# Rows of x2 for experts 2 to 31: fetched by indirect DMA from DRAM in place of selection on TensorE

## What is computed

```python
hn = rms_norm(x2, g)
g_prob = softmax(hn @ w_route_group + b_route_group); g_w, g_idx = top_k(g_prob, 1)
e_logits = (hn @ w_route_expert + b_route_expert).reshape(N, 4, 8)[arange(N), g_idx[:, 0]]
top_l, top_i = top_k(e_logits, 2)
comb = g_w * softmax(top_l)              # weights of the two experts of a row
eid = g_idx * 8 + top_i
# for each expert e and the rows xb that chose it:
y = (silu(xb @ w_gate[e]) * (xb @ w_up[e])) @ w_down[e]
out = x2 + sum over the two experts of y * comb
```

## Time and profile before

| | us |
|---|---|
| median of 3 runs | 989.34 (986.97 to 989.44) |
| profiled execution | 990.02 |
| its span | 987.9 |
| TensorE busy | 957.2 (97%) |
| VectorE busy | 405.5 (41%) |
| ScalarE busy | 245.5 (25%) |
| GpSimd busy | 58.5 (6%) |
| moved by DMA | 251.94 MB, mean 255 GB/s |

### The profile page before, as it was taken

The page is one execution under the profiler, slowest core; times in us unless marked ns, Lnnn a source line. Parts: engine busy times, 40 slices in busy tenths (PEclk is TensorE's granted clock), DMA queues, the critical chain, the costliest instruction groups (busy, mean ns, idle before and its releaser), DMA issues.

```text
span 987.9 us, 12620 instructions
## 1 busy us (share of the span) xinstructions
PE 957.2 (97%) x4944; PEld 520.3 (53%) x4944; DVE 405.5 (41%) x930; ACT 245.5 (25%) x607; POOL 58.5 (6%) x63
## 2 busy tenths in 40 slices
PE   5999999999999999999989999999999999999996
PEld 4554777777678888855453333333333333333332
DVE  4689688686543444562751241211211211111110
ACT  3432555355433100032212111111111111111110
POOL 0100000000000000001000101011101101101101
PEclk9999999999999999999999999999999999999998
DMA  9620412112112227288079999999999999999981
GB/s 327 212 86 20 151 63 74 44 49 81 43 43 86 85 86 275 88 334 342 33 268 370 417 418 406 417 417 421 421 416 419 424 415 418 422 419 417 426 329 17
DMA packets 32537, 251.94 MB, mean 255 GB/s; under 512 B 7784, under 2 KB 11112, under 8 KB 17480
## 3 DMA queue, kind: packets, MB, share of 16 engines
q1 hardware_dynamic: 28768, 242.19, 60.4%
q0 software_dynamic: 3712, 8.96, 3.6%
HBM read 244.08 MB, written 12.35 MB: 260 GB/s over the span
## 4 chain that ended last, share of the span: by engine, by line
PE 89%; DVE 6%; DMA 2%; ACT 1%; issue 1%; SPq 1%; POOL 0%; POOLq 0%; DVEq 0%; ACTq 0%
PE ps L1954 24%; PE ps L2258 21%; PE ps L2285 12%; PE ps L2198 10%; PE ps L1892 6%; PE ps L2113 4%; DMA arena<-in_x 2%; PE ps L2243 2%; PE ps L2268 1%; PE ps L2039 1%; PE ps L2013 1%; PE ps L1970 1%; PE ps L1996 1%; PE ps L2259 1%; PE ps L2147 1%
## 5 line engine op out<-in xcount | busy, mean ns | idle before, releaser
L1954 PE MATMUL ps<-arena 128*128 128x272 f32 x1120 | 266.7, 394 | 2.6 <-DVE arena L1368 1.0
L1954 PEld LDWEIGHTS ps<-arena 128*128 128x128 f32 x1120 | 209.0, 190 | 52.2 <-issue 7.0
L2259 PE MATMUL ps<-arena 128*64 128x512 f32 x512 | 226.5, 595 | 0.0
L2258 PE MATMUL ps<-arena 128*64 128x512 f32 x512 | 226.5, 595 | 0.0
L808 ACT ACTIVATE arena<-ps 128x272 f32<-128x272 f32 (+5 forms) x188 | 90.4, 487 | 387.6 <-PE ps L1954 168.4
L2258 PEld LDWEIGHTS ps<-arena 128*64 128x64 f32 x512 | 67.6, 137 | 126.5 <-issue 124.5
L2198 PE MATMUL ps<-arena 128*64 128x512 bf16 (+2 forms) x768 | 105.6, 424 | 2.9 <-DVE arena L1614 2.0
L1694 DVE SCALAR_TENSOR_TENSOR arena<-arena,list_w,ps 64x512 f32<-64x512 f32 x32 | 24.0, 749 | 201.5 <-ACT arena L1079 201.5
L1892 PE MATMUL ps<-arena 128*128 128x512 f32 (+1 forms) x192 | 74.9, 549 | 6.4 <-DVE arena L1160 6.4
L2198 PEld LDWEIGHTS ps<-arena 128*64 128x64 bf16 (+2 forms) x768 | 49.0, 117 | 52.3 <-issue 19.4
L1690 DVE TENSOR_TENSOR arena<-ps,g_ffn 128x512 f32<-128x512 f32 x32 | 22.1, 692 | 122.0 <-PE ps L2243 122.0
(11 more groups left out here) (258 smaller groups left out, 761.4 us busy)
## 6 DMA issues: line engine op xcount, KB each, us to landing
arena<-in_w_gu SPq DMA_DIRECT2D x62, 2048.0 KB, 16.7
arena<-in_w_ed SPq DMA_DIRECT2D x30, 2048.0 KB, 19.6
arena<-in_w_pair SPq DMA_DIRECT2D x20, 1024.0 KB, 4.9
arena<-in_w_q SPq DMA_DIRECT2D x2, 2048.0 KB, 15.5
arena<-in_w_out SPq DMA_DIRECT2D x2, 2048.0 KB, 12.3
arena<-in_w_ed SPq DMA_DIRECT2D x8, 512.0 KB, 14.1
arena<-in_w_gu SPq DMA_DIRECT2D x8, 512.0 KB, 17.3
arena<-in_x SPq DMA_DIRECT2D x4, 512.0 KB, 11.2
```

The source lines that it names most:

```text
L1954: ins = mm(out, w[:, k, :], tokens[:, k, :], start=k == 0 and q in "127", stop=k == 3, skip_group_check=q not in "127")
L2258: mm(ps[0:C, 2 + s, :], xT[s][:, j, :], w[:, jj, 1, :], start=j == 0, stop=j == JX - 1)
L2259: ins = mm(ps[64:64 + C, 2 + s, :], xT[s][:, j, :], w[:, jj, 0, :], start=j == 0, stop=j == JX - 1)
```

## The change

x2 is written a second time, to a DRAM tensor x2_rows, next to each store to y and by the same engine. For experts 2 to 31 the rows are fetched from it by an indirect DMA of GpSimd (gather_x) with the same list as the later add: 64 list entries, one row of 1024 values to one partition, entries beyond the list skipped. The two buffers x_rows lie on partitions 0 to 63 and 64 to 127 and are zeroed once. gather_x(2) and gather_x(3) are issued once all copies of x2 and the lists are there, gather_x(e + 4) in turn e of GpSimd's loop, once the rows of expert e + 2 have been transposed, before add_y(e). select_rows, hot_places and stage_x remain for experts 0 and 1 alone. turn_gathered transposes the 64 rows in eight steps of 128 columns in the place of turn_x's four. Semaphore counts follow; three semaphores are merged into zeros_set. The item loop still selects.

```diff
@@ -49,6 +49,7 @@
 NOBODY = 1024
 N_CHUNK = 10
 BIAS = 4096
+GATHERED = tuple(range(2, NE))
 UNROLL = 10
 MASKED = -1.0e30
 NEVER = -3.0e38
...
@@ -234,6 +235,7 @@
         hot = split(area(52608, 2 * (NT - 1) * C // 2).bitcast(BF16), (2, NT - 1, C))
         hot_last = area(52864, 2, C)
         mark_tmp = area(52992, NT, NE)
+        x_rows = [area(52992, D)[64 * s:64 * s + C, :] for s in range(2)]
 
 
         CHUNK_AT = [8192] + [19584 + 4096 * c for c in range(6)] + [0, 4096, 15488]
...
@@ -271,6 +273,8 @@
             at, n = CONST[name]
             return split(const[:, at:at + n], shape or (n,))
 
+        x2_rows = nc.dram_tensor("x2_rows", (T, D), F32, kind="Internal").ap()
+
         ident = cc("ident")
         before_bf, ones_bf = (cbf[:, n * P:(n + 1) * P] for n in range(2))
 
...
@@ -545,6 +548,10 @@
             upper, middle, lower = (split_rows[:, ORDER[j], n, c * 512:(c + 1) * 512] for n in range(3))
             return [(x_half(h), rest, upper, middle, lower)]
 
+        SELECTED = [e for e in range(NE) if e not in GATHERED]
+        N_SELECTED = len(SELECTED)
+        PER_ROUND = sum(UNROLL < e - 1 <= 2 * UNROLL for e in SELECTED)
+
         SELECT = [[(0, 0)]] + [[(j, n) for n in range(3)] for j in range(1, NT - 1)] + [[(NT - 1, 0)]]
 
         def x_bank(s):
...
@@ -588,9 +595,9 @@
         def base_written(eng):
 
             for b in range(4):
-                eng.wait_ge(half_moved[b], 48 if b < 3 else 16)
-            eng.wait_ge(last_written, 16)
-            eng.wait_ge(dec_written, 16)
+                eng.wait_ge(half_moved[b], 80 if b < 3 else 32)
+            eng.wait_ge(last_written, 32)
+            eng.wait_ge(dec_written, 32)
 
         block = ctx.enter_context(nc.Block())
 
...
@@ -682,6 +689,7 @@
             sp.wait_ge(out_ready, LAST + 1)
             load_chunk(EARLY + 1)
             sp.wait_ge(x2_ready, LAST + 1)
+            sp.dma_start(half_cols(x2_rows, LAST), x_half(LAST)).then_inc(last_written, 16)
             sp.dma_start(half_cols(o["y"], LAST), x_half(LAST)).then_inc(last_written, 16)
             load_chunk(N_CHUNK - 1)
 
...
@@ -755,17 +762,20 @@
             pool.wait_ge(c21_taken, 4)
             pool.dma_start(o["up_T"], uT[:, :, UP + SEQ - UP:UP + SEQ]).then_inc(nu_out, 16)
             pool.tensor_copy(split(u_decT.rearrange("p k n -> p (k n)"), (KD, DEC_B, DEC_S)),
-                             uT[:, :, UP + SEQ:].rearrange("p k (b u) -> p k b u", b=DEC_B)[:, :, :, UP:]).then_inc(u_dec_copied, 1)
-            pool.wait_ge(u_dec_copied, 1)
+                             uT[:, :, UP + SEQ:].rearrange("p k (b u) -> p k b u", b=DEC_B)[:, :, :, UP:]).then_inc(zeros_set, 1)
+            pool.wait_ge(zeros_set, 7)
             pool.dma_start(o["us_T"], u_decT).then_inc(nu_out, 16)
 
+            pool.memset(area(52992, D), 0.0).then_inc(zeros_set, 1)
             pool.wait_ge(x2_ready, 1)
+            pool.dma_start(x2_rows[SEQ:, :], x_dec[0:DEC, :]).then_inc(dec_written, 16)
             pool.dma_start(o["y"][SEQ:, :], x_dec[0:DEC, :]).then_inc(dec_written, 16)
             for h in range(1, LAST):
                 pool.wait_ge(x2_ready, h + 1)
+                pool.dma_start(half_cols(x2_rows, h), x_half(h)).then_inc(half_moved[(h - 1) % 4], 16)
                 pool.dma_start(half_cols(o["y"], h), x_half(h)).then_inc(half_moved[(h - 1) % 4], 16)
                 if 1 < h < 5:
-                    pool.wait_ge(half_moved[h - 2], 16)
+                    pool.wait_ge(half_moved[h - 2], 32)
                     pool.wait_ge(turned, h)
                     pool.wait_ge(ssq2_ready, h)
                     pool.wait_ge(parts_taken, h)
...
@@ -778,12 +788,22 @@
                     in_=y_rows[s][0:C, :], in_offset=None, compute_op=ALU.add,
                     bounds_check=T - 1, oob_is_err=False).then_inc(y_out[s], 16)
 
-            pool.wait_ge(dec_written, 16)
-            for bb in range(4):
-                pool.wait_ge(half_moved[bb], 48 if bb < 3 else 16)
-            pool.wait_ge(last_written, 16)
+            def gather_x(e):
+
+                pool.indirect_dma_start(
+                    out=x_rows[e % 2][0:C, :], out_offset=None, in_=x2_rows,
+                    in_offset=bass.IndirectOffsetOnAxis(ap=list_i[:, e:e + 1], axis=0),
+                    bounds_check=T - 1, oob_is_err=False).then_inc(x_full[e % 2], 16)
+
+            base_written(pool)
             pool.wait_ge(rows_listed, 1)
-            for e in range(NE):
+            pool.wait_ge(zeros_set, 8)
+            for e in range(-2, NE):
+                if e + 4 in GATHERED:
+                    above(pool, xe_ready, max([g + 1 for g in GATHERED if g < e + 4 and g % 2 == e % 2], default=0))
+                    gather_x(e + 4)
+                if e < 0:
+                    continue
                 for q in range(2):
                     pool.wait_ge(y_taken[q], e + 1)
                 above(pool, y_out[(e + 1) % 2], 16 * ((e + 1) // 2))
...
@@ -1088,18 +1108,24 @@
                 act.sem_inc(passed, 1)
                 copy(y_rows[s][0:C, 512:1024], ps[64:64 + C, 6 + s, :]).then_inc(y_taken[1], 1)
 
-            def stage_x(e, s, bank=0):
-
-                act.wait_ge(picked, e + 1)
-                above(act, xe_ready, e - 1)
-                copy(x_picked[s], ps[:, bank, :]).then_inc(x_staged, 1)
+            def stage_x(turn, free, bank=0, s=None):
+
+                act.wait_ge(picked, turn + 1)
+                above(act, xe_ready, free)
+                copy(x_picked[turn % 2 if s is None else s], ps[:, bank, :]).then_inc(x_staged, 1)
+
+            def stage(e):
+
+                turn = SELECTED.index(e)
+                stage_x(turn, SELECTED[turn - 2] + 1)
 
             stage_x(0, 0)
-            stage_x(1, 1, 3)
+            stage_x(1, 0, 3)
             do_silu(0, 0, root_of(0))
             take_hidT(0, 0)
             do_silu(1, 1, root_of(1))
-            stage_x(2, 0)
+            if 2 in SELECTED:
+                stage(2)
             base_written(act)
             take_y(0, 0, 0)
             for e in range(2, NE):
...
@@ -1703,11 +1730,12 @@
             def column(table, e):
                 return table[0:C, 0, e:e + 1] if isinstance(e, int) else table[0:C, 0, bass.ds(e, 1)]
 
-            def step(e, k, half, last=False):
+            def step(e, k, half, first=0, more=0, last=False):
 
                 s = k % 2
-                if not last and (not isinstance(e, int) or e > 1):
-                    hot_places(e + 1, 1 - s)
+                if not last and k + 1 + first in SELECTED:
+                    turn = SELECTED.index(k + 1 + first)
+                    hot_places(e + 1, turn + more, turn % 2)
                 if last:
                     take_y(e - 1, 1 - s, half - (1 - s))
                 hidden(e, s, column(list_w, e))
...
@@ -2234,14 +2263,28 @@
                 pe.wait_ge(sem, value)
                 pe.sem_inc(passed, 1)
 
-            def turn_x(e, s):
-
-
-                before_transposing(x_staged, e + 1)
-                rows = x_picked[s]
+            def turn_x(s, turn, part):
+
+
+                before_transposing(x_staged, turn + 1)
                 for j in range(JX // 2):
-                    ins = transpose(split(ps[:, x_bank(s), :], (2, JX // 2, C))[:, :, j, :], rows[:, j * P:(j + 1) * P], ident)
+                    ins = transpose(split(ps[:, x_bank(s), :], (2, JX // 2, C))[:, :, j, :], x_picked[part][:, j * P:(j + 1) * P], ident)
                 ins.then_inc(xe_ready, 1)
+
+            def turn_gathered(e, s):
+
+                pe.wait_ge(x_full[s], 16 * len([g for g in GATHERED if g <= e and g % 2 == s]))
+                rows, own = split(x_rows[s], (JX, P)), slice(64 * s, 64 * s + C)
+                for j in range(JX):
+                    ins = transpose(ps[:, x_bank(s), j * C:(j + 1) * C], rows[:, j, :], ident[own, own])
+                ins.then_inc(xe_ready, 1)
+
+            def turn_rows(e):
+
+                if e in GATHERED:
+                    turn_gathered(e, e % 2)
+                else:
+                    turn_x(e % 2, SELECTED.index(e), SELECTED.index(e) % 2)
 
             def gate_up(e, s, n, more):
 
...
@@ -2286,17 +2329,18 @@
                                  start=j == 0, stop=j == JH - 1)
                 ins.then_inc(dn_ready, 1)
 
-            turn_x(0, 0)
+            turn_rows(0)
             select(1, (NT - 1,), 3).then_inc(picked, 1)
             tile_list(NT - 1)
             gate_up(0, 0, up_no(0, 0), (0, 0))
             pe.wait_ge(rows_listed, 1)
-            turn_x(1, 1)
+            turn_rows(1)
             pe.wait_ge(hit_ready, NT + 1)
             list_rows(ps[0:C, 4, 0:2 * NE], 1, 2)
             gate_up(1, 1, up_no(1, 0), (0, 0))
             turn_hid(0, 0)
-            select_rows(2, 0)
+            if 2 in SELECTED:
+                select_rows(2, 0)
             for t in range(NT):
                 r = ROWS[t]
```

(50 more changed lines are left out.)

3 lines of the change are left out of this document (1 added, 2 removed).

## The result

The changed kernel takes 996.59 us (median of 4 runs, 995.62 to 997.55), the kernel before 988.89 us (4 runs, 986.97 to 989.44): a ratio of 1.0081, with the 95% interval 1.0062 to 1.0100. It is nearly 8 us slower. The forecast was 982.1 us, 7 us faster; the time lies outside the range of 978.5 to 991. The profiled execution took 995.84 us with a span of 994.0 us.

The account below looks back on a forecast made before the run. The weight stream was taken as the bound: its end, 961 - 1.0 (hole) + 9.6 (gathers) + 0.7 (add_y) = 970.3 us, plus the tail gave a span of 980.7 and a forecast of 982.1 us, range 978.5 to 991.

Parts of the forecast that it names:

- the lag: At the kernel's end: 20 us from the stream's last data to TensorE's last matmul, all a faster TensorE can win.
- TensorE's side: Expert loop: selection matmuls go, eight transposes take 0.78 us; an expert falls from 14.60 to 11.8 us.
- The gathers: Weight stream in the expert loop: 28 paid gathers at 0.34 us each move its end by 9.6 us.
- the bound above: Price of a gather in the expert loop: at most an indirect add's 0.73 us, 20.4 us for 28.
- Rival A: Expert loop: gathers dearer than their bytes, through uneven engine load or an add's cost; 992.9 us at the add's price; chance 0.25.
- Rival E: Expert loop: a gather is late or the additional queue traffic disturbs the weights; above 993 us; chance 0.05.
- The rule on accumulating transfers: Gather price: an accumulating transfer is half as fast as a copy, so a gather costs half an add, 0.36 us.
- The copies, the holes, the added waits: Before and early in the expert loop: copies cost 0, a closing hole gains 1.0 us, added waits cost nothing.
- The tail: After the last weight piece at 970.3 us: last matmuls end at 974.1 us, 6.65 us more to the span's end.
- Rival B: TensorE's clock falls while it waits for weights; a lag at the end of up to 4 us, 986 us; chance 0.12.
- C: Whole expert loop: the stream isn't the bound and TensorE's 84 us count in full, 905 us; chance 0.01.
- D: Kernel's end and expert loop: the tail runs at full clock and gathers sit more in gaps, 979 us; chance 0.05.

Follow-up runs that it names:

- e1_none: The changed kernel without the gathers for experts 4 to 31 (output not the layer's): 971.17 us, ratio 0.981 to the kernel before.
- e2_copies: The kernel before with only the second copy of x2 to DRAM added, nothing read from it: 988.59 us, ratio 0.9998.
- e6_spread: The changed kernel with each gather replaced by a plain load of 32 neighbouring rows, 1 KB to each of 128 partitions (wrong output): 979.2 us.
- e9_halves: The changed kernel with each gathered row sent as two half rows to partitions p and 64 + p, right output: 982.42 us, ratio 0.9931.

## Why the prediction was wrong

**What bounds the kernel.** Right. The weight stream was the slower resource, TensorE waits for it from about 620 us on (forecast 650; with the true 16.26 us per expert, 5.4 us a piece, the same working gives n = 32 and 637 us), and of 84 us taken from TensorE nothing was left beyond the lag.

**TensorE's side.** Right. Eight transposes take 0.64 us (forecast 0.78), an expert 11.7 us.

**The gathers: the term that failed.** "28 x 0.34 = 9.6 us". A gather cost not 0.34 us but 0.81 to 0.83 us, some 23 us in all, over the bound above of 20.4 us as well. The stream's end was forecast at 970.3 us and came at 984. Of the 13.7 us between, the gather's own engine time is a small part: 7.1% of 350 us less 22 adds at 0.73 us leaves 8.8 us for 22 gathers, 0.40 us each, if an add still takes what it took before; 28 x 0.06 = 1.7 us. The large part is what no term stood for, the weight packets beside it: (2.413 - 2.348) us per MB x 6.29 MB = 0.41 us per expert, 28 x 0.41 = 11.5 us. The sum so mended is 983.5 us. Per gather that is 0.81 us, and the ends say the same: 0.83 us from 984 - 961 + 1.0 - 0.7 over 28, 0.81 us from the last packets of the changed kernel and of e1_none, 984.6 - 962.0 over 28. The reasoning "less than its bytes it can't cost" was sound as a bound below. The bound above was not one: I took the price of an add as the worst, but an add writes to DRAM and takes its rows out of SBUF, and so could say nothing of writes into SBUF.

The Trainium skill ("SBUF — State Buffer", section "Door 1: The DMA port swizzle (why `[64,N]` ≈ `[32,N]`)") says that DMA bandwidth depends on how many of 16 ports the partitions reach, and that partitions 0 to 63 reach eight of them. The page says this of a transfer's own bandwidth. The runs fit it and go further, to the packets of the other queue: 633 ns beside loads to 32 partitions and 614 ns beside loads to 128. They show that the choice of partitions decides; that the two streams meet at the ports is an inference that no run here shows. Nor do they tell the number of partitions from the half in which they lie, since no load went to 32 partitions taken from both halves, or to all 64 of one; and the packet records don't name the DMA engine, so whether the slowed packets are those of some engines alone stays open.

**Rival A** had the right direction, place and turning point, and a chance of 0.25. It said that a gather over 0.60 us takes the gain away and over 0.70 us makes the kernel slower by more than 0.3%; it was 0.81 to 0.83 us, and 996.6 us came of it. Its mechanism was not this one. I looked for uneven load or a dear gather in q0's own time, and answered it with "the adds have the same shape and leave the total share at 1.01". The share is 1.01 after the change too, at 407 GB/s in the place of 418: here time in which packets are held up counts as busy, so the share can't show it. MB per share can. Of the signs of being wrong, this rival's came true (last data after 977 us, a period above 16 us).

**Rival E** named what happened, in one clause: "the additional queue traffic disturbs the weights: above 993 us". It had a chance of 0.05, no mechanism, no price and no sign of its own but a wait at the transposes for x_full, which belongs to its other half and did not come. So the disturbance was thought of, and the sum put it at nothing without giving a reason.

**The rule on accumulating transfers**, which the prediction took from the Trainium skill ("Collectives: The Full Stack", section "The bandwidth ceiling: the fold count and why AG ≠ RS ≠ AR"), held: 0.40 us for a gather against 0.73 us for an add, and by the packet records of the kernel before 159 ns for 4 KB of a plain transfer between 427 and 500 us against 328 ns for 4 KB of an add in the loop. It priced q0's time and nothing else.

**The copies, the holes, the added waits.** Right where the runs can tell: e2_copies costs nothing, gathers land in 8.6 us, and no wait for x_full is among TensorE's. The 1.0 us of the hole that closes was not tested by itself; without gathers the terms give 960.7 us, and the stream of e1_none ends at 962.0.

**The tail.** About 3 us from the last data to TensorE's end (forecast 3.8) and 6.9 us to the end of the span (forecast 6.65). The last 16 matmuls took 3.68 us at full clock, not the 5.4 us of the sum, a term mis-sized by 1.7 us that hides a little of the stream's error.

**Rival B**, the clock, is out: the mean granted clock from 600 to 950 us is 0.97 with all those waits, so they did not bring it to half each time, and the last down() ran at full clock. In e1_none the last down() did run at half clock (5.38 us), at a price of 1.7 us.

**C and D of the prediction.** C, the whole 84 us, did not happen; the floor is e1_none's 971 us. D was a fast tail and gathers in gaps: the tail was fast, but gathers in gaps would have cost less than 0.34 us.

## What to carry to other kernels

When two resources are full, a change that moves work from one to the other is worth at most the lag between their ends; work it out first, and then move only as much as makes both ends meet: four gathers of whole rows gained 1.3%, six in half rows 1.5%, thirty of whole rows lost 0.8%. Price a transfer that runs beside a full stream by what it does to the stream's own packets, and ask where it writes: gathers of 0.14 MB that landed on 34 partitions of one half cost more than twice what their bytes did (0.81 against 0.33 us). The share of busy DMA engines doesn't show this; compare MB per share of the stream's queue before and after.

## What the runs showed of the hardware that was not expected

0.13 to 0.14 MB per expert, written to 32 (or the first 34 of 64) partitions beside a stream that moves 420 GB/s without it, lengthens the stream's 16 KB packets from 614 to 631 to 633 ns on average over the loop, whether the rows are gathered or neighbouring, from the copy or the input, in pieces of 4 KB or 1 KB. The packets that start 4 to 8 us after a gather's issue bear it, with a mean of up to 761 ns. Written to all 128 partitions (e6_spread) or to 34 in each half (e9_halves), the same data lengthen them by nothing (614 ns). In the runs at 614 ns the indirect adds, which read SBUF and write DRAM, ran beside the stream all the time. A queue with 46 to 49 us of weights in it delivers them at the same rate as one with 11 to 27 us.
